# Convolution taps placed ahead of the group merge, the first expert weight subtraction and the first two gather indices moved to VectorE

## What is computed

```python
m_all = jnp.maximum(jnp.maximum(maxes[0], maxes[1]), maxes[2])
wts = [d_g * jnp.exp(m_g - m_all) for m_g, d_g in zip(maxes, dens)]
att = (wts[0][..., None] * outs[0] + wts[1][..., None] * outs[1]
       + wts[2][..., None] * outs[2]) / w_sum[..., None]
```

## Time and profile before

| | |
|---|---|
| runs | 2878.28, 2877.38, 2882.2 us |
| profiled execution | 2876.92 us, span 2875.1 us |
| TensorE busy | 2785.0 us (97%) |
| VectorE, ScalarE, GpSimd busy | 1788.3, 1250.4, 473.5 us |
| mean granted TensorE clock | 0.991 |
| experts | about 956 to 1517 us of the span |
| windowed attention | about 1729 to 2320 us; group 0 from 2105 us |

### The profile page before, as it was taken

One profiled execution on the slowest core, in us unless ns is written; L12 is line 12 of the kernel. 1 busy time (PEld: TensorE's weight loads), 2 busy tenths in 40 slices (PEclk: granted clock), 3 DMA queues, 4 the chain that ended last, 5 costly groups with the idle time before them and its releaser, 6 DMA issues.

```text
span 2875.1 us, 36993 instructions
## 1 busy us (share of the span) xinstructions
PE 2785.0 (97%) x14740; PEld 2327.5 (81%) x14740; DVE 1788.3 (62%) x2506; ACT 1250.4 (43%) x2019; POOL 473.5 (16%) x427
## 2 busy tenths in 40 slices
PE   8999999999999999999997999999999999999998
PEld 7978888867885788888887887878878768888898
DVE  4645888321445788888884877877677665110564
ACT  4234887232220677777776124454443443011101
POOL 1500131000000212111104000000000064231241
PEclk9999999999998999999998999999999999999999
DMA  4130000421115999999984121030210311110131
GB/s 144 49 135 16 30 1 1 163 87 67 59 59 193 369 391 395 393 392 397 396 323 147 59 90 58 19 114 27 72 55 27 99 64 45 59 44 30 51 141 59
DMA packets 141991, 382.33 MB, mean 133 GB/s; under 512 B 11759, under 2 KB 45041, under 8 KB 141692
## 3 DMA queue, kind: packets, MB, share of 16 engines
q1 hardware_dynamic: 125564, 324.17, 29.8%
q0 software_dynamic: 13520, 46.28, 5.1%
q10 hardware_dynamic: 2736, 9.50, 0.9%
HBM read 340.47 MB, written 39.46 MB: 132 GB/s over the span
## 4 chain that ended last, share of the span: by engine, by line
PE 71%; DVE 6%; ACT 2%; issue 1%; DMA 1%; POOL 1%; ACTq 0%; POOLq 0%; DVEq 0%; SPq 0%
PE ps L2784 7%; PE ps L2786 7%; PE ps L2785 7%; PE ps L2769 6%; PE ps L2771 6%; PE ps L2770 6%; PE ps L2399 4%; PE ps L2864 2%; PE ps L2866 2%; PE ps L2865 2%; PE ps L2913 2%; PE ps L2413 2%; PE ps L2878 2%; PE ps L2880 1%; PE ps L2879 1%
## 5 line engine op out<-in xcount | busy, mean ns | idle before, releaser
L2173 DVE SCALAR_TENSOR_TENSOR b_f<-b_f,small_f 128x1023 f32<-128x1023 f32 (+14 forms) x240 | 304.3, 1268 | 67.4 <-ACT small_f L1242 38.8
L2784 PE MATMUL ps<-x_f32r,w_f32r 128*128 128x512 f32 x480 | 187.5, 391 | 0.9 <-issue 0.8
L2786 PE MATMUL ps<-x_f32r,w_f32r 128*128 128x512 f32 x480 | 186.9, 389 | 0.0
L2770 PE MATMUL ps<-w_f32r,a_f32r 128*128 128x512 f32 x456 | 177.4, 389 | 0.0
L2785 PE MATMUL ps<-ht_f32r,w_f32r 128*128 128x512 f32 x416 | 161.9, 389 | 0.0
L2865 PE MATMUL ps<-w_f32r,a_f32r 128*128 128x512 f32 x384 | 149.9, 390 | 0.0
L2399 PE MATMUL ps<-small_f 128*128 128x128 f32 (+1 forms) x912 | 125.2, 281 | 25.2 <-DMA b_f<-acc 11.6
L2399 PEld LDWEIGHTS ps<-small_f 128*128 128x128 f32 (+1 forms) x912 | 107.1, 142 | 33.8 <-DMA b_f<-acc 12.0
L2770 PE MATMUL ps<-x_f32r,a_f32r 128*128 128x512 f32 x312 | 121.6, 390 | 0.0
L1158 POOL TENSOR_TENSOR w_f32r<-w_f,w_f32r 128x2048 fp32r<-128x2048 f32 x23 | 109.5, 4760 | 1.9
L1242 ACT ACTIVATE x_f<-ps 128x512 f32<-128x512 f32 (+1 forms) x184 | 91.3, 533 | 42.5 <-PE ps L2399 17.7
(11 more groups left out here) (526 smaller groups left out, 8017.7 us busy)
## 6 DMA issues: line engine op xcount, KB each, us to landing
w_f<-in_w_exp_up SPq DMA_DIRECT2D x40, 1024.0 KB, 9.3
w_f<-in_w_exp_down SPq DMA_DIRECT2D x38, 1024.0 KB, 8.0
w_f<-in_w_exp_gate SPq DMA_DIRECT2D x36, 1024.0 KB, 8.0
x_f<-in_w_exp_gate SPq DMA_DIRECT2D x28, 1024.0 KB, 7.7
x_f<-in_w_exp_down SPq DMA_DIRECT2D x26, 1024.0 KB, 9.4
x_f<-in_w_exp_up SPq DMA_DIRECT2D x24, 1024.0 KB, 9.5
w_f<-in_w_in SPq DMA_DIRECT2D x22, 1024.0 KB, 5.0
w_f<-in_w_in SPq DMA_DIRECT2D x10, 2048.0 KB, 7.9
```

The source lines that it names most:

```text
L2173: ins = v.scalar_tensor_tensor(C_conv[k][:, d:S], U_conv[k][:, 0:S - d], cols[:, k, R_TAP + j:R_TAP + j + 1], C_conv[k][:, d:S], ALU.mult, ...
L2770: mm(o, x1, w2[:, k, c], start=False, stop=False)
L2784: mm(o, l1, r1, start=(k == 0), stop=False)
L2786: ins = mm(o, l2, r1, start=False, stop=(k == n - 1))
```

## The change

- `LO_POOL` is empty: unit 0's low part is made by VectorE in its loop, ahead of unit 1's.
- VectorE writes `idx_g[0]` and `idx_g[1]` itself, each by an addition of one column, just before it writes `idxT`. `gather` makes the index copy only for e >= 2.
- GpSimd's wait for `flip` now stands behind the two gathers.
- `conv_share`: at `v` 4 taps in the groups 2 and 1 and 5 in group 0 (2 before); at `values` u = 3 in group 0 1 tap (5 before). The steps that had none still have none.

```diff
-        LO_POOL = [0]
+        LO_POOL = []
...
             if kind == "v":
-                return 2 if next_group(i) is None else 0
+                return (5 if tiles2[i][0] == 0 else 4) if next_group(i) is None else 0
             if kind == "scores" and u == 1:
                 return 2
             if kind == "values" and u == 3:
-                return 0 if i + 1 < len(tiles2) and next_group(i + 1) is not None else 5
+                return 0 if i + 1 < len(tiles2) and next_group(i + 1) is not None else (1 if tiles2[i][0] == 0 else 5)
...
                 if e >= 2:
                     bk.wait(pool, ("xT", e - 2, 1))
-                nc.gpsimd.tensor_copy(idx_g[par], idxT[:, e:e + 1]).then_inc(sem("idx_g"), 1)
+                    nc.gpsimd.tensor_copy(idx_g[par], idxT[:, e:e + 1]).then_inc(sem("idx_g"), 1)
                 pool.wait_ge(sem("idx_g"), e + 1)
...
             pool.wait_ge(sem("acc_out"), 16 * T)
-            bk.read(pool, ("flip",))
             gather(0)
             gather(1)
+            bk.read(pool, ("flip",))
...
             ch(v.tensor_tensor(idx_d, idx_d, sel, ALU.mult))
+            for e in range(2):
+                v.tensor_tensor(idx_g[e], idx_d[:, e:e + 1], idx_b[:, e:e + 1], ALU.add).then_inc(sem("idx_g"), 1)
             bk.done(v.tensor_tensor(idxT, idx_d, idx_b, ALU.add), ("flip",))
```

## The result

The changed kernel takes **2859.99 us** (median of 5 runs, 2858.63 to 2863.14), the kernel before 2878.28 us (5 runs, 2874.86 to 2882.2): a ratio of 0.9941 with the interval 0.9929 to 0.9953. The forecast was 2862.9 us, in a range of 2859.5 to 2869. The profiled execution went from 2876.92 to 2859.99 us, its span from 2875.1 to 2858.2, so there are 16.9 us to explain where 15.4 were forecast. (The medians lie 18.3 us apart, because the profiled execution before was 1.4 us under its median.) The total hides two errors: group 0 gave more than its term, the experts' start less.

What follows compares the result with a forecast made beforehand. TensorE, busy 97% of the span, was taken as the bound, so only its waits count. Group 0's 10.4, 0 for earlier groups and 5.0 at the experts' start gave 15.4 us: 2862.9 us, range 2859.5 to 2869.

Steps and rivals of the forecast that it cites:

- Part 1: Group 0: with four taps gone from behind the merge, all twelve TensorE waits for the exponentials go, 10.4 us.
- The air: Group 0: TensorE's turn would be ready 3.4 us before it is asked for.
- the 10.4 us: TensorE's twelve recorded waits for ScalarE's exponentials in group 0, all forecast to go.
- Part 2: Groups 2 and 1: 35.8 us of extra VectorE taps at `v` fit in idle time; effect 0.
- the chunk DMAs on ScalarE's queue keep their distance: Chunk DMAs stay two blocks or more behind the tap they wait for, before the chunk is needed; cost 0.
- Part 3: Experts' start: without GpSimd's subtraction beside it, VectorE's cast is done in time and TensorE's 1.09 us wait goes.
- Part 4: Experts' start: gather issued 3.4 us earlier, TensorE's 2.23 us wait goes, clock stays full; 5.0 us together with Part 3.
- the first rival: Experts' start: gather's issue held behind VectorE's subtraction, start gives 1.2 us, total 11.6 us, 2866.7 us; chance 0.14.
- I take the first: Experts' start: chose that VectorE's subtraction does not hold the gather's issue, giving 5.0 us, with 1.2 as lower end.
- The three terms 3.3 + 0.9 + 0.8: Experts' start: `xT` transposes 3.3 us earlier, 0.9 from there to the first product, 0.8 in its first five steps.
- my own mark: Experts' start: gather's issue near 945 us shows the forecast right; at 947 us it is wrong.

Runs made afterwards that it cites:

- E6: The changed kernel with 6 instead of 4 taps at `v` in groups 2 and 1: 2867.96 us, ratio 0.997.
- E3: The changed kernel with 2 instead of 4 taps at `v` in groups 2 and 1, group 0 as changed: 2866.49 us, ratio 0.9962.
- E5: E4 with 4 instead of 26 spare transposes on TensorE ahead of the indices: 2854.89 us, ratio 0.9923.
- E4: The changed kernel, but VectorE's subtraction for unit 0 waits until GpSimd has issued both first gathers: 2858.37 us, ratio 0.9936.
- E9: The kernel before with VectorE writing the first two index columns and the `flip` wait behind the gathers, unit 0 still on GpSimd: 2877.42 us, one run.
- E1: The kernel before with only the new `conv_share` (the taps) from the change: 2862.47 us, ratio 0.9948.
- E7: The changed kernel with 3 taps at `v` and 3 behind the merge in group 0, instead of 5 and 1: 2861.21 us, ratio 0.9946.
- E8: The kernel before with only unit 0's subtraction moved to VectorE: 2880.1 us, one run.

## Why the prediction was right, and where it was not

**Part 1, the taps of group 0: mechanism right, size short.** No wait for L1664 is left and the maxima start 0.5 us behind the scores, as was to be seen. The idle time before the merge was to be near 3 us and is less, 0.17 us in block 17 and 2.00 in block 18: used up but hardly overdrawn. The air was forecast at 3.4 us; the first exponentials are done at about 2142.4 and the turn begins at 2145.66, 3.2 us. The term mis-sized is the 10.4 us, which measured 13.1. I had taken TensorE's recorded idle time. That counts from the modelled end of the last product, and product records of 0.39 us follow each other every 0.227; a turn cut in two also takes 0.66 + 0.66 us where the whole one takes 1.03. TensorE in block 18 before, on both sides of the turn:

```profile
2149.22 0.39 PE L2866 MATMUL ps<-c_f32r,a_f32r 128*128 128x512 f32 x1
...
2152.69 0.47 PE L2878 MATMUL ps<-b_f32r,a_f32r 128*128 128x512 f32 x1
```

The last product before the turn starts at 2149.22, so the turn could start at 2149.45 and the next product 0.79 us behind that, as it does after (2145.66 to 2146.45). It came at 2152.69: 2.45 us lost, of which 2.02 were recorded as idle. The block periods say the same, 27.19 to 24.74 us. Six blocks with 0.44 us each beyond the recorded idle time are the missing 2.7.

**Part 2, the earlier groups: cover right, value wrong.** The cost was 0 as forecast, with idle times of 1.1 us and more left, and E6 shows what happens without them. But the step "the chunk DMAs on ScalarE's queue keep their distance" held only because of these taps. I had counted them only as the place where the fourth tap of each tile had gone; E3 shows that without them the last return comes late and costs 5.4 us of wait; of the 7.3 us of span in E3, 1.5 stood before group 0 began and 5.8 came behind. Part 1 without part 2 would have given 13.1 us in its blocks and lost 5.8 of them at the end of the stage.

**Part 3, the cast: right.** 0.21 us, no wait, 1.1 us off the path. What it frees goes partly into spare transposes that were counted for the old cast, which I had read as "end at 942.88" without asking what they now delayed (E5).

**Part 4, the gather: wrong, the first rival came true.** The step that failed is "its 0.2 us and 0.2 us to GpSimd the issue is at about 945.15", with "I take the first" behind it: that the issue isn't held by VectorE's subtraction. It began at 945.60, since GpSimd started it 0.8 us after its signal, and lasted 2.43 us. I had let decide; those are plain DMA issues of 547 to 552 ns, and five of the seven do begin beside a tap with two inputs in SBUF (the one at 2197.57 lies beside a tap with one, and the last has no tap left beside it). Two things differ from the gather, the kind of issue and VectorE's operation, and a trace I had settles which one counts. The kernel before, GpSimd and VectorE at the change of group:

```profile
1903.70 0.54 POOL L1179 DMA_DIRECT2D num<-x_f  x1 [25.80 <-DVEq L2285]
```

```profile
1903.49 2.29 DVE L2185 TENSOR_TENSOR w_f32r<-w_f,c_f32r 128x2048 fp32r<-128x2048 f32 x1 [3.53 <-ACT x_f L1242]
```

Beside the very same kind of subtraction a plain issue is not held. An indirect one is, 16 times in ten kernels: a gather's issue that begins while a subtraction runs ends 0.8 to 1.0 us behind it (1.80 to 2.81 us long), one that begins clear of any takes 0.96 to 1.07. From the end of the issue to the landing it is 6.5 to 6.6 us in the kernel before, the changed one, E4 and E5, so the time for which the issue is held stands in full in the landing. The rows landed at 954.59, 1.6 us before the old 956.23, where 3.4 were forecast, the wait stayed at 1.87 of 2.23 us and the clock dropped to 0.63 behind it. The three terms 3.3 + 0.9 + 0.8 measured 1.6 + 0.4 + 0.8 (the transposes of `xT` start 1.64 us earlier, from them to the first product it is 3.82 us instead of 4.18, and the low clock ends sooner behind it). Less the 0.1 us of earlier arrival, parts 3 and 4 gave 2.6 us, between the rival's 1.2 and the forecast's 5.0. The rival was short by having the clock stay as it was; in this trace it came back sooner, 1.00 instead of 0.50 from 959 to 962 us. By my own mark (issue "near 945 us", wrong "at 947") the start of the row would have passed: a mark should name the end of an instruction that can be held.

**The total.** 13.1 + 2.6 + 1.0 of the unedited stages + 0.1 ahead of both = 16.8 us, rounding apart the 16.9 of the span, against 10.4 + 5.0 = 15.4. The result fell in the whole range, 0.5 us above its lower end, and below the 2860.5 to 2865 that I had given the forecast itself. Part of that is luck: errors of opposite sign (2.7 us too little in group 0, 2.4 too much at the start) nearly cancelled, and 1.1 us of the gain belong to no edit. With group 0 sized rightly and the gather as forecast, it would have been 18 us. Left open: what makes GpSimd's first indirect issue start 0.8 us after its signal (also in E4, with nothing beside it), what moves TensorE's arrival at the experts' start and the stages right behind the experts by 1 us and more between kernels with the same code there, and why the clock falls behind a wait in one trace and not behind the same wait in another.

## What to carry to other kernels

Price a removed stop of TensorE by the distance between equal work before and after it, not by the idle time in the trace, which came out short here (2.02 us recorded, 2.45 us lost in a block). Before valuing an edit at nothing, look for what is scheduled by the count it changes (here the tap after which a DMA is issued). Before comparing spans that differ by 1 or 2 us, look whether the clock fell at the same places: one such fall was 1.6 us here. And when a wait is shortened, look again at the filler that was sized for it: 22 spare transposes too many cost 2.3 us here, nearly as much as the whole start had gained.

## What the runs showed of the hardware

- GpSimd's issue of an indirect gather is held by a VectorE subtraction with two inputs in SBUF that is running when it starts: 1.80 to 2.81 us instead of 0.96 to 1.07 (part 4). A plain DMA issue beside the same subtraction is not (0.54 us). Only the start of the gather's issue is held: in the changed kernel its last 1.0 us ran beside the second subtraction, and the third gather's, which began at 957.02, ahead of the subtractions from 957.76, took 1.02 us. The Trainium skill (SBUF — State Buffer, "Who interferes with whom") says that such an instruction holds up GpSimd's reads of SBUF, and infers that a tensor_tensor leaves the writing of descriptors alone; the traces agree with the first (GpSimd's index copy, 2.09 us beside a subtraction and 0.20 alone), and nothing in them speaks against the second. A gather's issue is given 128 row indices that lie in SBUF and a plain one none, so that it is held while it reads them would fit both halves, but no run here shows it.
- The hold works the other way too: a cast of a 32x128 tile on VectorE took 0.21 us alone and 3.86 to 4.51 us beside GpSimd's subtraction of 4.55 us (E9, the kernel before, E1).
- What a wait costs behind itself is not fixed, because the granted clock falls behind it in some traces and not in others. The eight transposes behind it took 1.97 us after a wait of 2.23 (before and E1), 1.85 after 1.87 (the changed kernel), but 1.09 after 1.85 in E7, the time at full clock, with the same code there. After 0.49 and 0.55 us (E4, E5) it was 1.09 as well. In group 0 a block with the same waits took 27.2 us at a clock of 1.00 and 28.8 us where it fell to 0.66 (E8).
